# Gate and up as seven block products in place of eight, in a two-layer decoder step on one core

## The reference

```
h = rmsnorm(x, g_pre_ffn)                      # 544 x 1024
f = jax.nn.silu(h @ w_gate) * (h @ w_up)       # 544 x 2816, both weights 1024 x 2816
x = x + rmsnorm(f @ w_down, g_post_ffn)        # w_down 2816 x 1024
```

## Time and profile before

| what | value |
|---|---|
| median of three runs | 1397.78 us |
| the profiled execution: span, first to last instruction | 1397.8 us |
| PE busy, share of the span | 1359.0 us, 97% |
| DVE busy | 713.3 us, 51% |
| ACT busy | 454.8 us, 33% |
| mean granted TensorE clock | 0.986 |
| DMA | 119.09 MB, mean 85 GB/s |

### The profile page before, as it was taken

One profiled execution on the slowest core, in us unless ns is written; L12 is line 12 of the kernel. 1 busy time (PEld: TensorE's weight loads), 2 busy tenths in 40 slices (PEclk: granted clock), 3 DMA queues, 4 the chain that ended last, 5 costly groups with the idle time before them and its releaser, 6 DMA issues.

```text
span 1397.8 us, 25646 instructions
## 1 busy us (share of the span) xinstructions
PE 1359.0 (97%) x10681; PEld 1312.8 (94%) x10681; DVE 713.3 (51%) x887; ACT 454.8 (33%) x630; POOL 36.3 (3%) x60
## 2 busy tenths in 40 slices
PE   7999999989999999999979999999999999999997
PEld 6999888989999999999879998899999999999996
DVE  6856658386344444222377465765944444442225
ACT  4532124454222222222254511244522222232222
POOL 3000002000000000000020000020000000000000
PEclk9999998999999999999989999999999999999999
DMA  6323112213332233222343221132222322222221
GB/s 217 91 76 89 49 46 81 91 54 98 90 90 78 87 90 90 83 87 66 110 122 89 76 78 46 46 101 86 64 88 90 90 86 80 89 90 83 91 84 64
DMA packets 110473, 119.09 MB, mean 85 GB/s; under 512 B 4576, under 2 KB 107128, under 8 KB 110136
## 3 DMA queue, kind: packets, MB, share of 16 engines
q1 hardware_dynamic: 107456, 108.57, 25.6%
q0 software_dynamic: 2496, 8.27, 2.0%
q10 hardware_dynamic: 440, 1.09, 0.2%
HBM read 113.23 MB, written 4.69 MB: 84 GB/s over the span
## 4 chain that ended last, share of the span: by engine, by line
PE 89%; DVE 5%; ACT 3%; issue 2%; DMA 0%; ACTq 0%; DVEq 0%
PE ps L491 27%; PE ps L493 27%; PE ps L492 26%; PE ps L660 1%; DVE x L1168 1%; PE ps L663 1%; ACT h_hi L911 1%; DVE r_post L1152 1%; PE ps L703 1%; PE ps L678 1%; PE ps L521 1%; DVE y L1163 1%; PE ps L641 1%; DVE r_pre L1205 1%; PE ps L719 1%
## 5 line engine op out<-in xcount | busy, mean ns | idle before, releaser
L491 PE MATMUL ps<-h_hi,w_hi 128*128 128x272 f32 x2240 | 661.7, 295 | 21.3 <-DVE h_lo L1189 11.2
L493 PE MATMUL ps<-h_lo,w_hi 128*128 128x272 f32 x2240 | 649.3, 290 | 0.0
L492 PE MATMUL ps<-h_hi,w_lo 128*128 128x272 f32 x2240 | 647.1, 289 | 0.0
L491 PEld LDWEIGHTS ps<-h_hi,w_hi 128*128 128x128 f32 x2240 | 425.1, 190 | 32.0 <-ACT h_hi L911 22.6
L492 PEld LDWEIGHTS ps<-h_hi,w_lo 128*128 128x128 f32 x2240 | 427.3, 191 | 2.9 <-issue 2.5
L493 PEld LDWEIGHTS ps<-h_lo,w_hi 128*128 128x128 f32 x2240 | 424.3, 189 | 0.0
L1132 DVE TENSOR_TENSOR w_lo<-w_raw,w_hi 128x1024 fp32r<-128x1024 f32 (+1 forms) x208 | 244.9, 1182 | 276.2 <-ACT w_hi L892 274.2
L892 ACT ACTIVATE w_hi<-w_raw 128x1024 fp32r<-128x1024 f32 (+1 forms) x208 | 211.7, 1021 | 234.8 <-DMA w_raw<-in_w_down 146.0
L491 PE MATMUL ps<-f_hi,w_hi 128*128 128x272 f32 x704 | 204.2, 290 | 0.0
L493 PE MATMUL ps<-f_lo,w_hi 128*128 128x272 f32 x704 | 203.1, 289 | 0.0
L492 PE MATMUL ps<-f_hi,w_lo 128*128 128x272 f32 x704 | 202.4, 288 | 0.0
(11 more groups left out here) (177 smaller groups left out, 1141.2 us busy)
## 6 DMA issues: line engine op xcount, KB each, us to landing
w_raw<-in_w_in SPq DMA_DIRECT2D x52, 512.0 KB, 3.7
w_raw<-in_w_gate SPq DMA_DIRECT2D x44, 512.0 KB, 3.7
w_raw<-in_w_up SPq DMA_DIRECT2D x44, 512.0 KB, 3.7
w_raw<-in_w_down SPq DMA_DIRECT2D x36, 512.0 KB, 3.4
w_raw<-in_w_out SPq DMA_DIRECT2D x16, 512.0 KB, 3.4
w_raw<-in_w_down SPq DMA_DIRECT2D x16, 256.0 KB, 2.9
tab<-in_table POOLq DMA_DIRECT2D x2, 1536.0 KB, 6.4
st_s<-in_state_ret POOLq DMA_DIRECT2D x8, 256.0 KB, 4.7
```

The source lines that it names most:

```text
L491: pe.matmul(out, wh, hi[:, cols(half)], start=begins, stop=False)
L492: pe.matmul(out, wl, hi[:, cols(half)], start=False, stop=False)
L493: mm = pe.matmul(out, wh, lo[:, cols(half)], start=False, stop=ends)
```

## The change

For pairs 3 to 10 of each layer (`SEVEN_FROM = 3`), gate and up are no longer formed as the plain product of `h` (two token halves by two halves of 512 rows) with the weights (two halves of 512 rows by two column blocks of 128). They are formed by Winograd's form of Strassen's product: seven sums of blocks of `h` (`a_sum`), made once a layer, times seven sums of blocks of the weights, made for each projection, and seven products of 512 x 128 by 272, which PE adds up in three PSUM banks. A projection is 7 x 4 x 3 = 84 matmuls.

- The left side is scaled by norm and gain before it is split (`block`, `left_sum`, `a_split`, `left_low`), between the work of pairs 0, 1 and 2; those three pairs are now written out, and the loop has eight rounds.
- For each projection DVE makes four weight sums of 128 x 512 and seven low parts, ACT seven high parts (`low7`, `high7`). Five of the seven are made one unit ahead of PE (`LEAD7 = 5`): the high part m of the next unit goes to the same buffer `p_hi[m]` once product m of this unit is done.
- Bank 0 takes products 0, 2, 4 and 6 one upon another, bank 2 products 3 and 5, bank 1 product 1. Between two of them ACT or DVE reads the bank out (`take`): four reads by ACT into `part` and the result, three by DVE, which add or subtract. PE's first matmul of a product waits for such a read.
- A weight slot is freed by DVE, after the low part that reads it last (`low7`, m = 4 and 5), and no longer by PE.
- `f` is kept unsplit and is split in the down stage and in the last unit ahead of it (`f_split`, `f_low`: eleven of 128 x 1088 a layer on each engine, in place of 22 of 128 x 544). SBUF is laid out anew: `p_hi` lies over `w_hi`, the `a` tiles over `f_hi`, `f` over `h`.

The core of the diff:

```diff
+PAIRS = FT // 2
+SEVEN_FROM = 3
+LEAD7 = 5
+BANK7 = [0, 1, 0, 2, 0, 2, 0]
 # PE
+                def unit7(jj, i):
+                    for m in range(7):
 ...
+                        if m == 0:
+                            pe.wait_ge(act_took.sem, act_took_at(l, jj - 1, i, 4))
+                        if m == 1:
+                            pe.wait_ge(vec_took.sem, vec_took_at(l, jj - 1, i, 1))
+                        if m == 2:
+                            pe.wait_ge(act_took.sem, act_took_at(l, jj, i, 1))
 ...
+                        if m == 6:
+                            pe.wait_ge(vec_took.sem, vec_took_at(l, jj, i, 2))
+                        after(a_lo_made, m + 1)
+                        pe.wait_ge(p_lo_made.sem, p_lo_made.at(l, 14 * jj + 7 * i + m + 1))
+                        out = ps[:, 4 * i + BANK7[m], 0:H2]
+                        for k in range(4):
 ...
+                            pe.matmul(out, wh, hi, start=begins, stop=False, skip_group_check=True)
+                            pe.matmul(out, wl, hi, start=False, stop=False, skip_group_check=True)
+                            mm = pe.matmul(out, wh, lo, start=False, stop=ends, skip_group_check=True)
+                        mm.then_inc(product.sem, 1)
-                with pe.Fori(1, FT // 2) as j:
-                    ffn_pair(j)
+                with pe.Fori(0, PAIRS - SEVEN_FROM) as jj:
+                    for i in range(2):
+                        unit7(jj, i)
 # ACT
+                def high7(jj, i, m, first=False):
 ...
+                    act.activation(p_hi[m][:], right7(i, m), ACT.Copy).then_inc(p_hi_made.sem, 1)
+                def take(jj, i, m, n, dst):
+                    act.wait_ge(product.sem, product_at(l, jj, i, m))
+                    act.activation(dst, ps[:, 4 * i + BANK7[m], 0:H2], ACT.Copy).then_inc(act_took.sem, 1)
+                def unit7(jj, i, last=False):
+                    for m in range(7):
+                        if m == 1:
 ...
+                            take(jj, i, 0, 1, part[:, 0, :])
+                        if m == 3:
 ...
+                            take(jj, i, 2, 2, part[:, 1, :])
+                        if m == 4:
 ...
+                            take(jj, i, 3, 3, part[:, 2, :])
+                        if m < 2:
+                            high7(jj, i, m + LEAD7)
+                        elif not last:
+                            high7(*((jj + 1, 0) if i else (jj, 1)), m - 2)
+                        elif m in (2, 4):
+                            act.wait_ge(product.sem, product_at(l, jj, i, m - 1))
+                            split(l, DOWN0 + m // 2 - 1)
+                        else:
+                            f_split({3: 0, 5: 1, 6: 2}[m])
+                    if i == 0:
+                        take(jj, 0, 6, 4, E[0][:, 0, cols(1)])
+                        for half in range(2):
 ...
+                            act.activation(E[1][:, :, cols(half)], E[0][:, :, cols(half)], ACT.Silu)\
+                               .then_inc(silu_made.sem, 1)
+                    else:
+                        take(jj, 1, 6, 4, acc[:, 0, cols(1)])
 # DVE
+                def low7(jj, i, m):
 ...
+                    if m == 0:
+                        for kh in range(2):
+                            vec.wait_ge(w_landed[slots7(i)[kh]], landings7(l, jj, i, kh))
+                        vec.tensor_tensor(t1[:], b1[:, :, 0:P], b1[:, :, P:2 * P], ALU.add)
+                        vec.tensor_tensor(b1[:, :, P:2 * P], b1[:, :, P:2 * P], b2[:, :, P:2 * P], ALU.add)\
+                           .then_inc(sums_made.sem, 1)
+                    if m == 1:
+                        vec.wait_ge(sums_made.sem, sums_made.at(l, n + 1))
+                        vec.tensor_tensor(t2[:], t1[:], b2[:, :, P:2 * P], ALU.add).then_inc(sums_made.sem, 1)
+                    if m == 3:
+                        vec.wait_ge(sums_made.sem, sums_made.at(l, n + 2))
+                        vec.tensor_tensor(t2[:], t2[:], b2[:, :, 0:P], ALU.add).then_inc(sums_made.sem, 1)
+                    vec.wait_ge(p_hi_made.sem, p_hi_made.at(l, 14 * jj + 7 * i + m + 1))
 ...
+                    ins = vec.tensor_tensor(p_lo[m][:], right7(i, m), p_hi[m][:], ALU.subtract)
+                    ins.then_inc(p_lo_made.sem, 1)
+                    if m in (4, 5):
+                        vec.wait_ge(p_lo_made.sem, p_lo_made.at(l, 14 * jj + 7 * i + m + 1))
+                        vec.sem_inc(w_used[slots7(i)[m - 4]], 1)
+                def unit7(jj, i, last=False):
+                    dst = acc if i else E[0]
+                    for m in range(7):
+                        if m in (2, 5, 6):
+                            take(jj, i, m - 1, dst)
+                        if m < 2:
+                            low7(jj, i, m + LEAD7)
+                        elif not last:
+                            low7(*((jj + 1, 0) if i else (jj, 1)), m - 2)
+                        elif m in (2, 4):
+                            split(l, DOWN0 + m // 2 - 1)
+                        else:
+                            f_low({3: 0, 5: 1, 6: 2}[m])
+                    if i:
 ...
+                            gated(pair, half, bass.ds(jj * 2, 2))
```

More of the change, by code:

```diff
@@ L196, in build @@
+        t2 = sb("t2", [P, 4, P])
+        p_lo = [sb(f"p_lo{m}", [P, 4, P], F32R) for m in range(7)]
+        zone = at[0]
         h_hi = sb("h_hi", [P, KT, T], F32R)
         h_lo = sb("h_lo", [P, KT, T], F32R)
[L198 to L202, removed]
@@ L932, in post_half @@
                     pair_done(act, l, half, wide_done, 4 * norm + pair + 1, pos)
-                    if pair == 0 and norm and half == 0:
-                        after(f_lo_made, 22)
                     if pair >= 2:
@@ L1082, in ffn_pair @@
+                after(stored, stored.per)
+                for j in range(SEVEN_FROM):
+                    if j == 0:
                         pre_root_half(1, 0)
+                        split(l, FFN0 + 4, j)
+                        split(l, FFN0 + 5, j)
+                        pre_root_half(1, 1)
                     else:
@@ L1550, in ffn_pair @@
-                    for half in range(2):
-                        vec.wait_ge(f_hi_made.sem, f_hi_made.at(l, j * 2 + half + 1))
-                        vec.tensor_tensor(f_lo[:, bass.ds(j * 2, 2), cols(half)], acc[:, :, cols(half)],
-                                          f_hi[:, bass.ds(j * 2, 2), cols(half)], ALU.subtract)\
-                           .then_inc(f_lo_made.sem, 1)
-                after(stored, stored.per)
-                ffn_pair(0, True)
-                with vec.Fori(1, FT // 2) as j:
-                    ffn_pair(j, False)
+                        gated(j, half, f_slots(j))
@@ L1560, in _ @@
+                    if j == 0:
+                        block(0)
+                        block(1)
+                    if j == 1:
+                        left_sum(5)
+                        left_low(0)
+                        left_low(1)
+                with vec.Fori(0, PAIRS - SEVEN_FROM - 1) as jj:
+                    for i in range(2):
+                        unit7(jj, i)
+                unit7(PAIRS - SEVEN_FROM - 1, 0)
+                unit7(PAIRS - SEVEN_FROM - 1, 1, True)
                 for n, (pair, k0, nk) in enumerate(DOWN):
```

278 lines of the change are left out of this document (224 added, 54 removed).

## The result

The changed kernel takes 1357.62 us (median of four runs, 1356.28 to 1358.67) against 1397.51 us for the kernel before: ratio 0.9721, 95% interval 0.9707 to 0.9734. Predicted were 1352 us, in a range from 1346 to 1373. The profiled execution spans 1355.6 us and took 1357.17.

A forecast was written before the change was run, and what follows sets the result against it. PE was taken to bound the kernel, by number of matmuls times pace. 1397.8 - 48.3 (removed matmuls) + 2.2 (loop entry) + 0.6 (loop exit) = 1352.3 us; predicted 1352, range 1346 to 1373.

The forecast's parts named there:

- The removed matmuls: In gate and up projections of pairs 3 to 10: 12 fewer matmuls in each of 32, at 0.1258 us, save 48.3 us.
- No stall in the steady loop: In the eight-pair loop PE never waits for DVE or ACT; some 0.4 us is left at product 6, 0.3 at product 2.
- the walk: Up unit's DVE and ACT queues timed step by step: DVE reads product 4 from 8.09 to 8.53 us, PE wants product 6 at 9.06.
- The entry: At the loop's start DVE's backlog behind a weight load makes PE wait some 1.1 us a layer, 2.2 in all.
- The exit: In the last up unit DVE's read of product 4 stands behind a split: some 0.3 us a layer, 0.6 in all.
- The base: Starting time of the kernel before: profiled span 1397.8 us, taken as equal to the runs' median, 1397.78.
- rival B: DVE and ACT operations start only after the previous one ends: 1365 us, 1373 with doubled loop loss; 24% for both forms.
- Rival C: Many short waits lower TensorE's clock to 1.2 GHz in part of the loop: 1420 us with eight units slowed; chance 6%.
- Rival D: Twelve matmuls in a row into one bank slow PE's pace to 0.144 us, the gain is gone: 1398 us; chance 4%.

## Why the prediction was right, and where it was off

- **The removed matmuls, 48.3 us: right.** A loop without gaps takes 169.37 + 0.13 = 169.5 us against 193.28, 23.8 a layer and 47.6 in all. The pace is 0.1261 us, where 0.1258 was taken.
- **No stall in the steady loop: right, reserve included; how closely the walk met it is luck.** DVE's read of product 4 came within 0.01 us of the walk, but by two errors that cancel: low part 5 began 0.13 us early, behind an ACT that was quicker than charged, and DVE's wait for itself made the step to low part 6 1.10 us where the walk had 0.91. The 0.4 us left after the signal were right (9.08 - 8.52 - 0.16 = 0.40).
- **The entry, 2.2 us: right in place and mechanism, too small in size.** The gaps cost 1.82 + 2.16 = 4.0. In layer 1 the walk put the read's end 10.1 us after the loop's start, and it came at 376.72 - 366.07 = 10.65; the step from low part 5 to 6 lasts 1.12 where I took 0.74, for the wait of DVE for itself; and the 0.26 to PE's start come on top. Behind the gaps came what I had priced at nothing: 1.5 us at the lower clock in layer 2, and 0.1 for each restart.
- **The exit, 0.6 us: right in size** (2 x 0.28). That it could not be mended by moving the read alone was not foreseen.
- **The base.** I took the span of the profiled execution (1397.8 us) and the median of the runs (1397.78) for the same thing. A run's time is 1.57 us above its span (1357.17 and 1355.6), so by estimate that execution lasted 1399.4 us and was slower than the median. From span to span the change gave 42.2 us, from median to median 39.9, and 45.5 were forecast. In spans, 1352.3 was forecast and 1355.6 measured: 0.7 for the pace, 1.8 for the entry, 0.4 for restarts and 1.5 for the clock, less 1.1 that the stages outside the loops came out shorter, where the clock at 210 to 225 us happened to be 0.77 in place of 0.66.
- **The range.** The median lies 5.6 us above the forecast and within the range, which reaches so far up for the sake of rival B; B did not happen.
- **Rival B** is refuted: operations of 0.68 us start 0.60 apart on DVE, and two more of them cost 2 x 0.60, less the room of 0.40, plus 0.09 for PE's restart. The Trainium skill, page "VectorE: DVE Perf Modes", has it in "Two Vector instructions with no wait between them" that an instruction that is held starts only when all earlier ones have finished, and in its drain section that one that is not held starts earlier; this qualifies the rule that I had set beside the rival, and the 0.60 agrees with it. The Trainium skill's drain section also has it that a semaphore behind each operation costs nothing extra. The trace agrees where a signal is only raised (each low part raises one, and the next operation starts after 0.60); where DVE also waits for its own last operation, it shows 1.11 us.
- **Rival C** happened in small, not in the loop's many short waits but behind single gaps of some 2 us. With nine matmuls a product, where PE idles 2.2 us in each gate unit, it came within the loop too, in three single rounds of fourteen with such a gap: one is the 0.68 of full clock at 500 to 505 us. The Trainium skill's rule on small idle times between groups of matmuls ("TensorE: Matmul & The Clock Gate", "A second HAM failure mode: psum-queue depth-cycling") is not borne out at 0.64 us of idle time per 22.08: the clock stayed at 1.00.
- **Rival D** is refuted: twelve matmuls in a row on one bank stand 0.126 us apart.

## What to carry to other kernels

Where an engine is busy in all of a stage, taking work from it is worth its count times its pace (here 47.6 us, with 48.3 forecast), and what remains to be found out is whether the engines beside it keep up: walk the queue of the one whose load rises, by start-to-start times, to each read that the first engine waits for. Look hardest at the places where the steady order begins and ends, and at what an engine could do there while it waits for a load. When a wait is taken away, look for it one stage on before counting the gain.

## What the runs showed of the hardware that was not expected

- A gap of about 2 us in PE's work can cost 1.7 times its length: behind three of eight the granted clock fell (0.63 over 4.65 us in one), which cost 1.5 us beside the 2.16. Length alone did not decide it: behind 2.09 us it fell, behind 3.59 it did not.
- A DVE operation that waits for the one just begun, with a semaphore raised between, starts 1.1 to 1.25 us after it, where an independent one starts 0.60 after.
- PE starts 0.16 us after the end of the DVE read that it waited for in the up units, and 0.26 in nearly all gate units (why they differ is open), and its next matmul follows after 0.22 in place of 0.13 us.
